# A two-layer attention and expert kernel: gates, half of the latents and both attention output projections as three float32r terms

## The chip, the cores and the metric

The kernel runs on one core of one Trainium2 chip. The metric is device microseconds of that core for one execution. Engine names are those of the profile: PE is TensorE's matmul, PEld its weight load, DVE is VectorE, ACT is ScalarE, POOL is GpSimd, SP is the engine that issues most DMAs.

## The reference

Three blocks run on a 256 x 1024 float32 activation x. The first two are layers of one kind, and the change concerns them alone:

```python
proj = x @ w_in[i]                       # 1024 -> 3*512 + 768 + 256 + 32 + 2*1024
na_qkv, q_lat, kv_lat, k_rope, g_na, g_mla = jnp.split(proj, ...)
o_na  = neighborhood_attention(q_na, k_na, v_na, na_rpb[i])     # 8 heads of 64
q_mla = rms_norm(q_lat) @ w_uq[i]; kv = rms_norm(kv_lat) @ w_ukv[i]
o_mla = latent_attention(q_mla, k_mla, v_mla)                   # 8 heads
merged = sigmoid(g_na + b) * (o_na @ w_na_o[i]) + sigmoid(g_mla + b) * (o_mla @ w_mla_o[i])
x = layer_norm(ALPHA * x + merged @ w_out[i])
f = swiglu(x) if i == 0 else moe_swiglu(x)      # layer 1: 8 experts, 2 of them per token
x = layer_norm(ALPHA * x + f + sigmoid(x @ w_ple_gate[i]) * (p[i] @ w_ple[i]))
```

A third block with other mixers and a dense feed-forward follows.

## The kernel before

The five engines run programs of their own, each in a fixed order written out by hand, and meet at semaphores. Activations lie feature-major in tiles of 128 features x 256 tokens; a projection of 1024 inputs to 128 outputs is a "tile" of eight k-steps into one PSUM bank, and two banks each are shared between PE and ACT (`act_ps`) and between PE and DVE (`dve_ps`).

**Weights** come through `weight_ring`, 7 slots of 16 KB per partition (`SLOTS`, L81). A block of up to 2 MB fills a slot. SP issues the blocks in order (L657 to L660); block i waits until PE has finished block i-7. The experts' blocks go through the same 7 slots (L632 to L636): the first seven wait for the blocks that held the slots.

**Products** come in two kinds. `product` (L817 to L826) multiplies float32 by float32. `split_product` (L911 to L920) multiplies three float32r terms per k-step, short x short, short x rest and rest x short. "short" is the operand rounded to float32r, "rest" is what is left; a half slot (128 x 2048) is a unit. Its short comes from a cast into another buffer, its rest from a subtraction in place in the ring. In the layers, the queries, keys and values (split by DVE, `split_in_w`, L1777), `w_out` and `w_ple_gate` (`layer_units`: units 0, 1, 5 by POOL, the rest by DVE) and the dense feed-forward (`split_w`, L1802, by DVE) are products of three terms already. All latents, the gates, and the output projections `w_na_o` and `w_mla_o` are float32.

**Attention** takes 16 jobs per layer, first 8 neighbourhood heads (NA), then 8 latent heads (MLA), as a software pipeline over steps s = 0 to 17. The orders within a step are:

- PE (L866): scores of job s, the gate tile s as a filler (`gate_tile`, L1153), transposes of the probabilities of job s-1, values of job s-2.
- DVE (L1699): `maxima(s)` (L1720 or L1725, then the tiny L1726), `normalise(s-1)` (L1737, then two instructions of L1747), `output(s-2)` (L1758).
- ACT (L1365): the exponentials of job s, the read of gate tile s (L1498), the copy of the transposed probabilities of job s-1.

Call E(s) the moment at which PE ends gate tile s. After step 17 PE waits for the last output and goes on with the 8 tiles of `w_na_o` and the 8 of `w_mla_o`. DVE multiplies each by its gate (L2025; L2039 and L2040 for the second, then L2032 and L2036, which split the merged tile), and the three-term `w_out` follows.

**POOL** masks the bias table of layer 0 early (L692), waits for half of the attention's maxima, loads the next bias table, splits its three units of `w_out` and `w_ple_gate`, masks again, and is free until the experts, where it makes every sixth rest (L724).

## Time and profile before

| what | value |
|---|---|
| three runs | 2307.92, 2311.07, 2311.77 us; median 2311.07 |
| profiled execution | 2307.82 us, its span 2306.0 us |
| busy in the span | PE 2204.6, PEld 1870.1, DVE 1502.4, ACT 980.5, POOL 346.0 us |
| attention of layer 0, of layer 1 (gate tiles) | about 117 to 210 us, 622 to 715 us |
| output projections | about 216 to 244 us, 721 to 749 us |
| experts | about 839 to 1780 us |

How to read it: the span is one execution on the chip; the 1.8 us between it and that execution's own time lie around it. The median of the runs lies 3.25 us above the profiled execution. A busy share is an average over stages with different limits, so the stages that the change touches are read one by one below.

### The profile page before, as it was taken

Reading aid. Unit: us, or ns where it says so; the run is one execution under the profiler, and the core shown is the slowest. Engines: PE = TensorE matmul, PEld = TensorE weight load, DVE = VectorE, ACT = ScalarE, POOL = GpSimd, SP = SyncE. Lnnn points to the kernel's source line nnn. Section 1 sums busy time; section 2 is a strip of 40 time slices with the busy share of each in tenths; the row PEclk is TensorE's granted clock in tenths of the full one; section 3 lists DMA queues with packets and bytes.
Section 4 is the critical chain, followed back from the end, with each engine's and each line's share of the span. In section 5 each row is a group of like instructions: output and inputs, shape, how many; then the busy total and the mean of one; then the engine's idle time right before and its main releaser. Section 6 shows DMA issues by size and latency. Waiting matters only on the chain.

```text
span 2306.0 us, 29557 instructions
## 1 busy us (share of the span) xinstructions
PE 2204.6 (96%) x11972; PEld 1870.1 (81%) x11972; DVE 1502.4 (65%) x1489; ACT 980.5 (43%) x1043; POOL 346.0 (15%) x95
## 2 busy tenths in 40 slices
PE   8999999989999979999999999999999798969999
PEld 7777899989777868888888888888888586648998
DVE  4342677755333568898888898988889301445776
ACT  0133210010133257777777777778776203241000
POOL 1001200000001112322323223223243000100000
PEclk9999999999999989999999999999999996979999
DMA  9532578643513459999999999999999332303530
GB/s 341 183 124 73 170 268 294 237 132 115 180 60 110 165 209 381 372 384 367 384 367 384 366 385 371 385 374 380 384 387 343 132 135 84 110 0 110 183 128 19
DMA packets 176770, 552.20 MB, mean 239 GB/s; under 512 B 11264, under 2 KB 98944, under 8 KB 133280
## 3 DMA queue, kind: packets, MB, share of 16 engines
q1 hardware_dynamic: 167984, 516.77, 60.9%
q10 hardware_dynamic: 6912, 24.97, 2.7%
q0 software_dynamic: 1776, 9.08, 1.0%
q8 instruction: 71, 1.16, 0.2%
q14 instruction: 27, 0.22, 0.0%
HBM read 527.19 MB, written 23.59 MB: 239 GB/s over the span
## 4 chain that ended last, share of the span: by engine, by line
PE 90%; DVE 6%; ACT 2%; issue 1%; DMA 1%; POOL 0%; DVEq 0%; SPq 0%; ACTq 0%; POOLq 0%
PE act_ps L990 25%; PE act_ps L825 13%; PE dve_ps L1015 12%; PE dve_ps L825 9%; PE dve_ps L918 8%; PE act_ps L918 8%; PE job_ps L951 5%; PE job_ps L825 2%; DVE weights_rest L1884 2%; PE job_ps L877 2%; PE job_ps L998 1%; PE job_ps L888 1%; PE act_ps L1126 1%; ACT expert_short L1414 0%; DVE pre_norm L1673 0%
## 5 line engine op out<-in xcount | busy, mean ns | idle before, releaser
L1884 DVE TENSOR_TENSOR weights_rest<-weight_ring,expert_short 128x2048 fp32r<-128x2048 f32 x280 | 768.2, 2784 | 113.6 <-ACT expert_short L1414 113.6
L1414 ACT ACTIVATE expert_short<-weight_ring 128x2048 fp32r<-128x2048 f32 x336 | 640.8, 1917 | 115.1 <-PE act_ps L990 75.7
L724 POOL TENSOR_TENSOR weights_rest<-weight_ring,expert_short 128x2048 fp32r<-128x2048 f32 x56 | 267.4, 4776 | 685.6 <-ACT expert_short L1414 685.6
L990 PE MATMUL act_ps<-expert_short,tokens_short 128*128 128x512 f32 x896 | 355.1, 396 | 12.0 <-DVE tokens_rest L1894 12.0
L990 PE MATMUL act_ps<-weights_rest,tokens_short 128*128 128x512 f32 x896 | 350.0, 391 | 0.0
L990 PE MATMUL act_ps<-expert_short,tokens_rest 128*128 128x512 f32 x896 | 349.9, 391 | 0.0
L1330 ACT ACTIVATE arena_mla<-act_ps 128x256 f32<-128x256 f32 (+2 forms) x89 | 34.2, 385 | 419.5 <-PE act_ps L918 346.1
L990 PEld LDWEIGHTS act_ps<-expert_short,tokens_short 128*128 128x128 f32 x896 | 168.8, 188 | 46.1 <-issue 12.3
L990 PEld LDWEIGHTS act_ps<-expert_short,tokens_rest 128*128 128x128 f32 x896 | 168.8, 188 | 36.4
L990 PEld LDWEIGHTS act_ps<-weights_rest,tokens_short 128*128 128x128 f32 x896 | 169.0, 189 | 33.7
L1813 DVE TENSOR_TENSOR weights_rest<-weight_ring,ffn_weights_short 128x2048 fp32r<-128x2048 f32 x66 | 151.3, 2293 | 2.3
L918 PE MATMUL act_ps<-ffn_in_short,ffn_weights_short 128*128 128x256 f32 x480 | 140.3, 292 | 10.3 <-DVE ffn_in_rest L2215 4.7
L1015 PE MATMUL dve_ps<-expert_short,hidden_short 128*128 128x512 f32 x448 | 139.4, 392 | 0.0
L918 PE MATMUL act_ps<-ffn_in_rest,ffn_weights_short 128*128 128x256 f32 x480 | 138.2, 288 | 0.0
L1015 PE MATMUL dve_ps<-expert_short,hidden_rest 128*128 128x512 f32 x448 | 138.1, 389 | 0.0
L1015 PE MATMUL dve_ps<-weights_rest,hidden_short 128*128 128x512 f32 x448 | 138.0, 389 | 0.0
L918 PE MATMUL act_ps<-ffn_in_short,weights_rest 128*128 128x256 f32 x480 | 137.9, 287 | 0.0
L1811 DVE CAST ffn_weights_short<-weight_ring 128x2048 fp32r<-128x2048 f32 x66 | 80.9, 1225 | 61.7 <-PE act_ps L918 33.4
L825 PE MATMUL act_ps<-residual,weight_ring 128*128 128x256 f32 x512 | 117.4, 382 | 0.0
L825 PEld LDWEIGHTS act_ps<-residual,weight_ring 128*128 128x128 f32 x512 | 95.9, 190 | 17.8 <-issue 5.3
L918 PEld LDWEIGHTS act_ps<-ffn_in_short,ffn_weights_short 128*128 128x128 f32 x480 | 94.4, 197 | 13.4 <-issue 8.6
L713 POOL TENSOR_TENSOR weights_rest<-weight_ring,ffn_weights_short 128x2048 fp32r<-128x2048 f32 x6 | 27.1, 4526 | 505.6 <-ACT ffn_weights_short L1510 505.4
(323 smaller groups left out, 3958.3 us busy)
## 6 DMA issues: line engine op xcount, KB each, us to landing
weight_ring<-in_moe_w SPq DMA_DIRECT2D x336, 1024.0 KB, 6.9
weight_ring<-in_w_in SPq DMA_DIRECT2D x44, 1024.0 KB, 7.4
weight_ring<-in_ffn_w SPq DMA_DIRECT2D x32, 1024.0 KB, 7.1
weight_ring<-in_w_out SPq DMA_DIRECT2D x12, 1024.0 KB, 6.9
weight_ring<-in_w_gate SPq DMA_DIRECT2D x11, 1024.0 KB, 5.5
weight_ring<-in_w_up SPq DMA_DIRECT2D x11, 1024.0 KB, 8.0
weight_ring<-in_w_down SPq DMA_DIRECT2D x10, 1024.0 KB, 5.9
weight_ring<-in_w_ple_gate SPq DMA_DIRECT2D x8, 1024.0 KB, 6.8
```

The lines of the kernel that those rows point to most:

```text
L724: nc.gpsimd.tensor_tensor(ring_lo[slot][:, half], ring[:, slot, half], shorts[u % SHORTS][:, :], ALU.subtract)\
L825: m = nc.tensor.matmul(out, lhs[k], rhs[k], start=first and k == 0, stop=last and k == len(lhs) - 1)
L877: m = nc.tensor.matmul(out, j["q"][:, i * P:(i + 1) * P], j["k"], start=True, stop=True)
L918: m = nc.tensor.matmul(out, a[:, k, at], x_parts[x_part][:, k, :], start=(k == i == 0), stop=(k == DT - 1 and i == 2))
L951: m = nc.tensor.matmul(acc(j), w[:, k, at], ff_h[h][:, pair % 4, k, :], start=(pair == k == i == 0 and j % 2 == 0), stop=(2 * pair + k == ...
L990: m = nc.tensor.matmul(bank[0:CAP, :], a[:, 4 * c + k, :], w[:, k, :], start=(c == k == i == 0), stop=(c == 1 and k == 3 and i == 2))
L1015: m = nc.tensor.matmul(dve_ps[n_half][0:CAP, :], h[:, g % 2, 2 * c + k, :], w[:, k, n_half * 512:(n_half + 1) * 512], start=(g == c == k = ...
L1330: nc.scalar.activation(out, bank[rows, 0:width], func, **kw).then_inc(act_tile_done, 1)
L1414: nc.scalar.activation(shorts[u % SHORTS][:, :], ring[:, slot, half], ACT.Copy).then_inc(moe_w_short, 1)
L1811: V.tensor_copy(ff_w[u % 2][:, :], ring[:, block % SLOTS, half]).then_inc(ffn_w_short, 1)
L1813: V.tensor_tensor(ring_lo[block % SLOTS][:, half], ring[:, block % SLOTS, half], ff_w[u % 2][:, :], ALU.subtract)\
L1884: V.tensor_tensor(ring_lo[slot][:, half], ring[:, slot, half], shorts[u % SHORTS][:, :], ALU.subtract)\
```

## The change

The change leaves the mathematics as it is and turns more products into the three-term kind:

- The latents' last block (4 of 8 tiles per layer), all 16 gate tiles and all 16 tiles of the two output projections become `split_product`s: 14 new units per layer, `side_units`.
- Weights: the casts of layer 0's units 0 and 1 are ACT's; all other casts and all 14 subtractions of a layer are POOL's (`split_side`). Units 0 and 1 are the latents', 2 to 9 the gates' (two tiles each), 10 and 11 `w_na_o`, 12 and 13 `w_mla_o` (four tiles each). From unit 4 on POOL waits until PE is done with unit u-2; units 11 to 13 wait for the last gate tile.
- Heads: DVE splits pairs of heads (`split_heads`: a 128 x 256 cast and a subtraction) between the steps of attention, at steps 10 to 15 and 17.
- Room: outside the experts the ring has 5 slots. Slots 5 and 6 hold the split of x (`in_x`) and the two shorts (`side_w`). Block i now waits for block i-5. The first two of the experts' blocks that go into slots 0 to 4 wait for `w_ple` and for the first block of `w_ple_gate`, the third waits for the second block of `w_ple_gate`, and SP issues all later ones behind it.
- x is split by DVE before the copies of the latents rather than between them. `w_out`'s unit 1 takes `side_w[0]` as its short, and ACT's cast for it waits for unit 10.

Cut to its core:

```diff
+LAYER_SLOTS, SIDE_UNITS = 5, 14
...
-        in_x = [parts("layer_in_short", "probs", [P, DT, SEQ]), parts("layer_in_rest", "arena_o", [P, DT, SEQ])]
+        in_x = [parts("layer_in_short", "weight_ring", [P, DT, SEQ], SLOT * LAYER_SLOTS),
+                parts("layer_in_rest", "weight_ring", [P, DT, SEQ], SLOT * LAYER_SLOTS + 2048)]
+        in_x_flat = [a[:, :, :].rearrange("p k s -> p (k s)") for a in in_x]
+        o_short = [parts(f"heads_short{i}", "arena_gate", [P, 4, SEQ], 1024 * i) for i in range(2)]
+        o_rest = [parts(f"heads_rest{i}", "arena_o", [P, 4, SEQ], 1024 * i) for i in range(2)]
+        side_w = [parts(f"side_weights_short{b}", "weight_ring", [P, 2048], SLOT * (LAYER_SLOTS + 1) + 2048 * b) for b in range(2)]
...
-            out += [(halves(panel(w, COL_GATE + 512 * i, COL_GATE + 512 * (i + 1))), "AAAA") for i in range(4)]
-            out += [(halves(panel(t["w_na_o"][l], 0, D)), "D" * DT), (halves(panel(t["w_mla_o"][l], 0, D)), "D" * DT)]
+            out += [(panels_at(w, COL_GATE + 512 * i), "AAAA") for i in range(4)]
+            out += [(column_halves(t["w_na_o"][l]), "D" * DT), (column_halves(t["w_mla_o"][l]), "D" * DT)]
...
+        def side_units(l):
+
+
+            units = []
+            for u in range(SIDE_UNITS):
+                block, c = (queries_at[l] - 1, u) if u < 2 else (ple_block_at[l] - 8 + (u - 2) // 2, u % 2)
+                a, d = tiles_before[block]
+                units.append((block, c, (dve_tile_ready, d + 2 * (c + 1)) if u < 2 else
+                              (act_tile_ready, a + 2 * (c + 1)) if u < 10 else (dve_tile_ready, d + 4 * (c + 1))))
+            return units
+
+        def side_short_of(u):
+
+            return side_w[u % 2] if u < 12 else in_x_flat[u - 12]
+
+        def layer_short_of(i):
+
+            return side_w[0] if i == 1 else ff_w[i % 2]
+
...
+            if block < before_moe:
+                return weights_here[slot], 32 * (block // LAYER_SLOTS + 1)
+            turns = len(range(slot, before_moe, LAYER_SLOTS)) + (block - before_moe) // LAYER_SLOTS + 1
+            return weights_here[slot], 32 * turns
+
+        def slot_of(block):
+
+            return (block if block < before_moe else block - before_moe) % LAYER_SLOTS
...
-                        sp.wait_ge(*blocks[before_moe - SLOTS + b][1])
+                        sp.wait_ge(*(blocks[max(range(b, before_moe, LAYER_SLOTS))][1] if b < LAYER_SLOTS
+                                     else layer_units(1)[1][2]))
...
+                if i >= LAYER_SLOTS:
+                    sp.wait_ge(*blocks[i - LAYER_SLOTS][1])
...
+            def split_side(l, u):
+
+                units = side_units(l)
+                block, c, _ = units[u]
+                half = slice(c * 2048, (c + 1) * 2048)
+                if (l, u) not in ((0, 0), (0, 1)):
+                    pool.wait_ge(*weights_landed(block))
+                    if u < 2:
+                        pool.wait_ge(*layer_units(l - 1)[1][2])
+                    else:
+                        pool.wait_ge(*units[min(u - 2, 9)][2])
+                    nc.gpsimd.tensor_copy(side_short_of(u)[:, :], ring[:, slot_of(block), half]).then_inc(side_short, 1)
+                pool.wait_ge(side_short, SIDE_UNITS * l + u + 1)
+                nc.gpsimd.tensor_tensor(ring_lo[slot_of(block)][:, half], ring[:, slot_of(block), half], side_short_of(u)[:, :],
+                                        ALU.subtract).then_inc(side_split, 1)
+
...
             for l in range(LAYERS):
-                pool.wait_ge(max_ready, layer_jobs * l + NA_H)
+                if l:
+                    for u in range(2):
+                        split_side(l, u)
+                for u in range(2, 8):
+                    split_side(l, u)
                 if l < LAYERS - 1:
+                    pool.wait_ge(max_ready, layer_jobs * l + NA_H)
                     load_bias(l + 1)
+                for u in range(8, SIDE_UNITS):
+                    split_side(l, u)
...
+                def side_weights(u):
+
+                    block, c, _ = side_units(l)[u]
+                    pe.wait_ge(side_split, SIDE_UNITS * l + u + 1)
+                    k = DT if u < 10 else 4
+                    return tiles(side_short_of(u)[:, :], k), tiles(ring_lo[slot_of(block)][:, c * 2048:(c + 1) * 2048], k)
+                for u in range(2):
+                    w = side_weights(u)
+                    for j in range(2):
+                        split_product(dve_bank()[:, 0:SEQ], w, slice(j * P, (j + 1) * P), in_x).then_inc(dve_tile_ready, 1)
+                n.block += 1
+
                 def in_weights(i):
 
...
-                    if s % 4 == 0:
-                        gate_w.append(weights(DT, 512))
-                    product(act_bank()[:, 0:SEQ], cols(gate_w[-1], s % 4 * P, (s % 4 + 1) * P), xs)\
+                    if s % 2 == 0:
+                        gate_w.append(side_weights(2 + s // 2))
+                    split_product(act_bank()[:, 0:SEQ], gate_w[-1], slice(s % 2 * P, (s % 2 + 1) * P), in_x)\
                         .then_inc(act_tile_ready, 1)
+                    if s % 4 == 3:
+                        n.block += 1
                 attention(layer_jobs * l, layer_jobs, gate_tile)
-                feature_tiles("D", weights(4, D), k_tiles(o_na, 4))
-                feature_tiles("D", weights(4, D), k_tiles(o_mla, 4))
+                for i in range(2):
+                    for c in range(2):
+                        w = side_weights(10 + 2 * i + c)
+                        for j in range(4):
+                            split_product(dve_bank()[:, 0:SEQ], w, slice(j * P, (j + 1) * P), (o_short[i], o_rest[i]),
+                                          (lambda k: (heads_split, DT * l + 4 * i + k + 1)) if c == j == 0 else None)\
+                                .then_inc(dve_tile_ready, 1)
+                    n.block += 1
                 layer_tiles(l, 0, "D", merged_parts, lambda k: (merged_split, DT * l + k + 1))
                 after = last_tiles(DT)
                 i = n.block
                 w_ple = weights(2, D)
-                p_l = tiles(ring[:, i % SLOTS, 2 * D:2 * D + 2 * SEQ], 2)
...
+            for block, c, _ in side_units(0)[0:2]:
+                act.wait_ge(*weights_landed(block))
+                nc.scalar.activation(side_w[c][:, :], ring[:, slot_of(block), c * 2048:(c + 1) * 2048], ACT.Copy)\
+                    .then_inc(side_short, 1)
...
-                    nc.scalar.activation(ff_w[i % 2][:, :], ring[:, block % SLOTS, c * 2048:(c + 1) * 2048], ACT.Copy)\
+                    if i == 1:
+                        act.wait_ge(*side_units(l)[10][2])
...
+                    if beside:
+                        beside(s)
...
+            def split_heads(l, i, j):
+
+                dve.wait_ge(out_copied, layer_jobs * l + NA_H * i + 2 * j + 2)
+                o = (o_na, o_mla)[i]
+                V.tensor_copy(o_short[i][:, j, :], o[:, j, :]).then_inc(heads_short, 1)
+                dve.wait_ge(heads_short, DT * l + 4 * i + j + 1)
+                V.tensor_tensor(o_rest[i][:, j, :], o[:, j, :], o_short[i][:, j, :], ALU.subtract).then_inc(heads_split, 1)
 
...
+                when = {10: ((0, 0),), 11: ((0, 1),), 12: ((0, 2),), 13: ((0, 3), (1, 0)), 14: ((1, 1),), 15: ((1, 2),), 17: ((1, 3),)}
+                attention(layer_jobs * l, layer_jobs, beside=lambda s: [split_heads(l, i, j) for i, j in when.get(s, ())])
```

## Rows read from the trace of the kernel before

**Rows 1.** The page: the chain that ended last, by engine

```profile
PE 90%; DVE 6%; ACT 2%; issue 1%; DMA 1%; POOL 0%; DVEq 0%; SPq 0%; ACTq 0%; POOLq 0%
```

**Rows 2.** The chain in layer 0: start us, us, what; an attention step, then the projections

```profile
156.08 0.44 PE job_ps L888 x4
...
158.58 3.65 PE act_ps L825 x16
...
170.70 3.46 PE act_ps L825 x16
...
212.05 0.63 DVE probs L1747 x2
...
215.67 27.89 PE dve_ps L825 x128
243.56 23.19 PE dve_ps L918 x192
```

**Rows 3.** Timeline of POOL, layer 0: start us, us, engine line op, releaser

```profile
266.90 1.89 POOL L709 CAST ffn_weights_short<-weight_ring 128x2048 fp32r<-128x2048 f32 x1 [36.97 <-PE dve_ps L918]
268.87 4.53 POOL L713 TENSOR_TENSOR weights_rest<-weight_ring,ffn_weights_short 128x2048 fp32r<-128x2048 f32 x1
```

**Rows 4.** Timeline of DVE, the same attention step, and two merging instructions

```profile
157.56 0.42 DVE L1758 COPY arena_o<-job_ps 64x256 f32<-64x256 f32 x1 [3.40 <-PE job_ps L825]
158.62 0.42 DVE L1720 CUSTOM_DVE_ANT_0 probs<-job_ps,arena_bias 128x256 f32<-128x256 f32 x1 [0.64 <-PE job_ps L877]
...
159.43 0.17 DVE L1726 TENSOR_SCALAR small<-small 128x2 f32<-128x2 f32 x1
...
159.70 0.61 DVE L1747 TENSOR_SCALAR probs<-probs,small 128x256 f32<-128x256 f32 x2
...
235.77 0.28 DVE L2032 CAST merged_short<-work 128x256 fp32r<-128x256 f32 x1
235.97 0.42 DVE L2036 TENSOR_TENSOR merged_rest<-work,merged_short 128x256 fp32r<-128x256 f32 x1
```

**Rows 5.** Timeline of POOL and DVE side by side, third block

```profile
1974.38 0.84 DVE L1747 TENSOR_SCALAR probs<-probs,small 128x256 f32<-128x256 f32 x2
...
1974.51 1.00 POOL L786 TENSOR_SCALAR arena_o<-arena_o,params_sb 128x256 f32<-128x256 f32 x1
...
1980.61 1.09 POOL L790 TENSOR_TENSOR arena_o<-arena_o,tmp 128x512 f32<-128x512 f32 x1
1980.83 0.89 DVE L1726 TENSOR_SCALAR small<-small 128x2 f32<-128x2 f32 x1
```

**Rows 6.** Timeline of DVE and POOL in layer 0: a cast behind the bias mask

```profile
43.62 8.88 POOL L692 TENSOR_TENSOR arena_bias<-arena_bias,consts_sb 128x3072 f32<-128x3072 f32 x1 [8.62 <-DMA arena_bias<-in_na_rpb]
...
48.01 5.58 DVE L1785 CAST layer_weights_short<-weight_ring 128x2048 fp32r<-128x2048 f32 x1 [2.20 <-PE act_ps L918]
```

**Rows 7.** Timeline of DVE: fourth latent tile, and a weight cast late in layer 0's feed-forward

```profile
22.61 0.42 DVE L1656 COPY work<-dve_ps 128x256 f32<-128x256 f32 x1 [3.03 <-PE dve_ps L825]
...
484.32 1.22 DVE L1811 CAST ffn_weights_short<-weight_ring 128x2048 fp32r<-128x2048 f32 x1
485.58 2.29 DVE L1813 TENSOR_TENSOR weights_rest<-weight_ring,ffn_weights_short 128x2048 fp32r<-128x2048 f32 x1
```

**Rows 8.** The page: weight DMAs, count, KB each, median us from issue to landing

```profile
weight_ring<-in_w_in SPq DMA_DIRECT2D x44, 1024.0 KB, 7.4
```

**Rows 9.** The chain ahead of the experts

```profile
817.53 8.54 PE act_ps L918 x48
...
829.74 5.50 ACT expert_short L1414 x3
```

**Rows 10.** Stretches: us, busy of PE, PEld, DVE, ACT, POOL, then granted clock, DMA share, GB/s

```profile
815.00:816.00 1.00, 0.00 (x0) 0.00 (x0) 0.00 (x0) 0.80 (x1) 0.53 (x1) 1.00 1.04 442
820.00:821.00 1.00, 1.00 (x7) 1.00 (x6) 0.96 (x3) 0.00 (x0) 0.00 (x0) 0.50 0.00 0
900.00:1000.00 100.00, 99.31 (x454) 81.99 (x453) 87.54 (x44) 77.19 (x53) 28.73 (x6) 1.00 0.98 380
```

More of the change, by code:

```diff
@@ L437, in two_panels, with column_halves, dmas, panels_at @@
             return pair_block(w, w, c0 // 256, c0 // 256 + 1)
+        def column_halves(w):
+            def dmas(slot):
+                return [(tiles(slot[:, i * 2048:(i + 1) * 2048], 4), panel(w, 512 * i, 512 * (i + 1))) for i in range(2)]
+            return dmas
+        def panels_at(w, c0):
+            def dmas(slot):
+                return [(tiles(slot[:, i * 2048:(i + 1) * 2048], DT), panel(w, c0 + 256 * i, c0 + 256 * (i + 1))) for i in range(2)]
+            return dmas
         def down_block(w2, g, f_tiles):
@@ L473, in layer_plan @@
             w = t["w_in"][l]
-            out = [(halves(panel(w, COL_LAT + c0, COL_LAT + c1)), "D" * ((c1 - c0) // P)) for c0, c1 in lat_blocks(l)]
+            out = [(halves(panel(w, COL_LAT + c0, COL_LAT + c1)) if i < len(lat_blocks(l)) - 1 else
+                    two_panels(w, COL_LAT + c0), "D" * ((c1 - c0) // P)) for i, (c0, c1) in enumerate(lat_blocks(l))]
             out += [(two_panels(w, COL_Q), "AAAA"), (two_panels(w, COL_K), "DDDD"), (None, "AA"),
@@ L618, in load @@
                 dmas, _ = blocks[i]
-                for dst, src in dmas(ring[:, i % SLOTS, :]):
-                    sp.dma_start(dst, src).then_inc(weights_here[i % SLOTS], 16)
+                for dst, src in dmas(ring[:, slot_of(i), :]):
+                    sp.dma_start(dst, src).then_inc(weights_here[slot_of(i)], 16)
             def load_expert_block(e, b, base):
@@ L708, in _ @@
                         pool.wait_ge(*units[i - 2][2])
-                        nc.gpsimd.tensor_copy(ff_w[i % 2][:, :], ring[:, block % SLOTS, half]).then_inc(pool_w_short, 1)
+                        nc.gpsimd.tensor_copy(layer_short_of(i)[:, :], ring[:, slot_of(block), half]).then_inc(pool_w_short, 1)
                         pool.wait_ge(pool_w_short, l + 1)
@@ L712, in _ @@
                         pool.wait_ge(act_w_short, 2 * l + i + 1)
-                    nc.gpsimd.tensor_tensor(ring_lo[block % SLOTS][:, half], ring[:, block % SLOTS, half], ff_w[i % 2][:, :],
+                    nc.gpsimd.tensor_tensor(ring_lo[slot_of(block)][:, half], ring[:, slot_of(block), half], layer_short_of(i)[:, :],
                                             ALU.subtract).then_inc(pool_w_split, 1)
@@ L913, in split_product @@
                 short, rest = w
-                for k in range(DT):
+                tiles_in = short.shape[1]
+                for k in range(tiles_in):
                     if after:
@@ L926, in layer_tiles @@
                     pe.wait_ge(*layer_unit_split(l, i))
-                    w = tiles(ff_w[i % 2][:, :], DT), tiles(ring_lo[block % SLOTS][:, c * 2048:(c + 1) * 2048], DT)
+                    w = tiles(layer_short_of(i)[:, :], DT), tiles(ring_lo[slot_of(block)][:, c * 2048:(c + 1) * 2048], DT)
                     for j in range(2):
@@ L942, in swiglu @@
                     half = slice(c * 2048, (c + 1) * 2048)
-                    short, rest = ff_w[u % 2][:, :], ring_lo[block % SLOTS][:, half]
+                    short, rest = ff_w[u % 2][:, :], ring_lo[slot_of(block)][:, half]
                     if kind == "w2":
@@ L1104, in in_weights @@
                     pe.wait_ge(in_w_split, 6 * l + i + 1)
-                    return tiles(in_w[i % 2][:, :], DT), tiles(ring_lo[block % SLOTS][:, c * 2048:(c + 1) * 2048], DT)
+                    return tiles(in_w[i % 2][:, :], DT), tiles(ring_lo[slot_of(block)][:, c * 2048:(c + 1) * 2048], DT)
                 for i in range(4):
@@ L1164, in _ @@
                 w_ple = weights(2, D)
-                p_l = tiles(ring[:, i % SLOTS, 2 * D:2 * D + 2 * SEQ], 2)
+                p_l = tiles(ring[:, slot_of(i), 2 * D:2 * D + 2 * SEQ], 2)
                 def embedding(j0, j1):
@@ L1509, in short_w @@
                     act.wait_ge(*weights_landed(block))
-                    nc.scalar.activation(ff_w[i % 2][:, :], ring[:, block % SLOTS, c * 2048:(c + 1) * 2048], ACT.Copy)\
+                    if i == 1:
+                        act.wait_ge(*side_units(l)[10][2])
+                    nc.scalar.activation(layer_short_of(i)[:, :], ring[:, slot_of(block), c * 2048:(c + 1) * 2048], ACT.Copy)\
                         .then_inc(act_w_short, 1)
@@ L1697, in rms_norm, with attention @@
                         .then_inc(rms_ready, 1)
-            def attention(first, count, fill=None):
+            def attention(first, count, fill=None, beside=None):
                 def maxima(a):
```

57 lines of the change are left out of this document (28 added, 29 removed).

## Prediction, made before the changed kernel ran

> **What bounds the kernel now.** I read the page's chain first: PE carries 90% of it [rows 1], so a PE saving is worth its full length unless something else becomes late. Then the chain in the stages that the change touches. In attention it is PE without a gap: transposes, values and scores take 2.50 us (156.08 to 158.58), then a float32 gate tile of 3.65 us with the neighbourhood heads and 3.46 us with the latent heads [rows 2]. Both output projections are 27.89 us without a gap, and the three-term `w_out` behind them 23.19 us for 8 tiles of 8 k-steps [rows 2]. Third, what DVE does within such a step [rows 4], since POOL's new work runs beside it, and what the two do to each other where they already meet [rows 5, 6].
>
> **What PE gains.** The float32 output projections are 64 k-steps in 27.89 us, 0.436 us each; `w_out` is 64 k-steps in 23.19 us, 0.362 us each [rows 2]. A three-term gate tile is then 8 x 0.362 = 2.90 us against 3.46: 0.56 us less. (The neighbourhood steps' extra 0.19 us I keep.) Sixteen gate tiles give 9.0 us a layer, the projections 64 x 0.074 = 4.7 us, four latent tiles 2.2 us. Both layers: 31.8 us, the whole of the hoped-for gain.
>
> **What POOL costs.** A unit is a cast of 1.89 us and a subtraction of 4.53 us, 6.5 us with the gap [rows 3]. PE uses a gate unit up in two steps, 11 us, so POOL is fast enough by itself. The question is DVE. L1726 works on 128 x 2 numbers and takes 0.17 us [rows 4], but 0.89 us when it starts in a POOL subtraction: it ends 0.02 us after it [rows 5]. DVE's 1.22 us cast [rows 7] took 5.58 us when it met POOL's mask: it ended 1.09 us after the mask did [rows 6]. So DVE's casts and its TENSOR_SCALAR from SBUF to SBUF wait for POOL's two-input instruction to its end. POOL can also step between two DVE instructions in a row: a pair of L1747 took 0.84 us for 0.61 with a POOL instruction started inside it [rows 4, 5].
>
> The Trainium skill, "SBUF — State Buffer", section "Who interferes with whom", says that such a pair of ports is held for the whole instruction of whoever came first. Rows 5 agree for the subtraction but not for POOL's 1.00 us TENSOR_SCALAR, which held DVE up by only 0.23 us. By the page POOL's casts block for their full 1.89 us, as below; if they held for that row's share only, the two in the tail below would cost some 3 us a layer less, and the sum would be about 2358.
>
> **A step of attention.** Let E be the end of a gate tile. From rows 2 and 4 with E = 156.08: DVE copies an output at E+1.48, starts the maxima at E+2.54, L1726 at E+3.35, L1747 at E+3.62 and ends it at E+4.23. PE needs that at the end of the next gate tile: E+6.15 now, E+5.59 after the change (E+5.40 with latent heads). The margin shrinks to 1.2 us. POOL starts a unit at an odd step's E, because PE then frees the buffer: cast to E+2.0, subtraction to E+6.6. L1726 waits from 3.35 to 6.6, and the remaining 0.9 us puts the probabilities at E+7.5: PE stalls 1.9 us (2.1 with latent heads). Units 4 to 8 do this: 3 x 1.9 + 2 x 2.1 = 9.9 us.
> At units 9 and 10 (steps 11, 13) DVE also has heads to split, a 0.28 us cast and a 0.42 us subtraction [rows 4], both blocked alike. The cast slips in between POOL's two instructions, the subtraction waits to E+6.8, the maxima start at 7.25 and 1.7 us later the probabilities are there: stall 3.5 us; with two splits at step 13, 4.2 us. Queued behind on DVE are the maxima, so ACT's exponentials come late too, but PE asks for them only a step later. Sum in attention 17.6 us a layer, against 9.0 gained.
>
> **The tail.** After E15 POOL has units 11, 12 and 13 and then two subtractions for `w_out`, 28 us with no pause, while DVE must finish. Chained as above: split cast in the gap (2.0 to 2.3), POOL subtraction to 6.8, split subtraction to 7.2, POOL cast to 9.1, first L1747 to 9.4, POOL subtraction to 13.9, second L1747 to 14.2. Today the pair starts at 212.05 and ends 2.8 us after E15, which is 170.70 + 3.46 plus six steps of 5.96 and thus 209.9 [rows 2]: 11.4 us lost. PE starts `w_na_o` at E+17.2; DVE's last head split is caught by units 13 and 14 and ends at E+25.9, and only then comes the gate product that frees PE's bank. PE has done two tiles by 20.1 and waits to 26.3: 6.2 us. With the 4.7 us gained the tail is +12.9 us. If POOL did not step between the L1747 pair it would be about +6; if nothing blocked, -4.7.
>
> **The start.** Layer 0's unit 0 needs block 2 (with x and the first blocks 5.2 MB, estimated landed at 18 to 19 us from the page's 341 GB/s of the first slice), ACT's cast (5.50/3 = 1.8 us [rows 9]) and 4.53 us on POOL: about 25 us. PE ends its fourth tile at 22.6 [rows 7]. Wait 2.4, gain 2.2: +0.2 us.
> Layer 1's units 0 and 1 need a block that is loaded when PE ends the feed-forward's fourth block from the end; it lands 7.4 us later [rows 8] and puts 13 us of POOL beside the last three weight splits of DVE, 3.5 us each [rows 7], which PE wants 5.8 us apart (48 matmuls of 0.121). A full chain of turns costs 9.5 us, a lucky one nothing; I take 5. With 2.2 gained: +2.8 us.
>
> **The ring.** Seven slots become five. Within the layers a block takes PE 11 us and DMA 7, so I cost it at nothing; the blocks ahead hide it. At the experts it shows: the third block is issued only when `w_ple_gate` is done, 826.1 [rows 9] (817.53 + 8.54), and both halves land some 7.5 us later, 833.5. ACT needs it for the second half of its shorts (from 829.74, 1.83 each [rows 9]: wanted at 831.6), and PE's start hangs on ACT. +1.9 us, between 0 and 5. After that PE takes 5.4 us per block and DMA gives 380 GB/s at a share of 0.98 [rows 10], so it keeps up, with little room.
> x's split moves ahead of the first latent copy: 3.5 us on DVE, hidden by PE's first tiles, done long before its fourth at 22.6 [rows 7]; late x could cost 1 us at most.
>
> **The clock.** After about 3 us in which PE was idle (815 to 816 wholly, until 817.53 [rows 9, 10]) the granted clock fell from 1.00 to 0.50, that is to 1.2 GHz [rows 10], and 48 matmuls took 8.54 us where 0.121 each makes 5.8 [rows 9]. Five stalls after the change are well over 3 us (two per layer in the tail, one in the feed-forward). I take 1.7 us each, between 0 and 2.7: +8.5 us.
>
> **Sum.** Per layer -9.0 + 17.6 + 12.9 = +21.5; twice 43.0; start 0.2 and 2.8; ring 1.9; clock 8.5: +56.4 us. On the profiled execution's 2307.8 us that is 2364 us. The median shown lies 3.3 us above that execution, which is inside what I can't resolve here.
>
> **Rivals.**
> A, *no harm*: POOL's instructions fall where they hold nothing up on DVE, and PE keeps its saving: -31.8, plus the ring's 1.9 and the start's wait of 2.4, is -27.5, 2280 us, faster than before. It decides at one point: whether POOL's subtraction is over by the time DVE's small L1726 plus the 1.2 us margin is up, E+4.6. POOL would have to finish 2 us sooner than rows 3 say, or DVE not to wait at all. Rows 5 and 6 speak against it; for it speaks only that they show short instructions and one cast, not a whole stage. 14%.
> B, *half the harm*: DVE waits at L1726 as in rows 5, but POOL does not step in between DVE instructions in the tail (+6 a layer, no long stall, no clock). 2 x (-9.0 + 14 + 6) + 5 = +27, 2335 us. 22%.
> C, *break-even*: B's stalls at the gates, but a tail that keeps its 4.7 us: 2 x (-9.0 + 14 - 4.7) + 5 is about +5, at the edge of no change, and a little less with fewer head splits caught. 6%.
> D, *the ring*: the experts start with an empty ring and DMA, at a share of 0.98, never fills it. Five blocks of 2 MB at 380 GB/s are 27 us, of which 13 pass before PE starts; up to 13 us more on top, 2377 us. 8%.
> The forecast, stalls plus tail plus clock: 50%.
>
> **How the numbers follow.** The predicted time is the forecast's. Range: 2310, below B, to 2390, above D with the clock at its upper bound; it leaves out A and most of C. A measurement of this kernel can tell 0.2% (4.6 us) from no change. Faster 0.15 (A and a sliver of C), same 0.05, slower 0.80.
>
> **What would show it.** In the changed profile: three-term gate tiles of 2.9 us; PE waiting at the transposes (L888's counterpart) for DVE's L1747 after every second gate tile, 2 us each; L1726 with a maximum of several us; L1747 too at the end of attention; PE idle before and inside `w_na_o`; granted clock below 1.0 in both tails. The forecast is wrong if L1726 stays near 0.2 us beside POOL's 4.5 us subtractions, or if the step of attention is 5.5 us throughout.

## The result, and the profile after

Four runs of the changed kernel took 2368.41, 2376.30, 2381.27 and 2382.16 us, median 2378.8, against 2309.5 for the kernel before beside them: 1.029 times its time, with a 95% interval of 1.026 to 1.033. The change makes the kernel 3% slower. The profiled execution is the first of the four; it is 60.6 us above that of before (2307.82).

The page's chain by engine, beside [rows 1]:

```profile
PE 85%; DVE 11%; ACT 2%; issue 1%; DMA 1%; POOL 0%; DVEq 0%; SPq 0%; ACTq 0%; POOLq 0%
```

Busy times of the engines (share of the span, instructions):

```profile
PE 2195.5 (93%) x12420; PEld 1874.7 (79%) x12420; DVE 1598.5 (68%) x1521; ACT 983.5 (42%) x1045; POOL 523.5 (22%) x149
```

PE is busy 9 us less than before and POOL 178 us more. In the chain DVE's share has nearly doubled, and POOL is as good as absent from it, though POOL is the cause: the chain names the engine whose instruction was long, not who held it up. Read alone, this row would send one to speed DVE up.

PE's waits, each with who ended them, total, count and longest:

```profile
PE job_ps L963 <- DVE probs L1849: 71.5, 22, 12.0
PE act_ps L1066 <- DVE tokens_rest L2006: 14.2, 1, 14.2
...
PE job_ps L1027 <- DVE weights_rest L1925: 9.0, 1, 9.0
```

The first wait is at the transposes, for the normalised probabilities. It grew from 13.9 us, 8 times, longest 2.6. L963 is the transposes (L888 before), L1828 the tiny negation (L1726), L1849 the normalisation (L1747).

One step of attention, DVE's timeline and then POOL's, beside [rows 4]:

```profile
146.63 0.42 DVE L1822 CUSTOM_DVE_ANT_0 probs<-job_ps,arena_bias 128x256 f32<-128x256 f32 x1
...
147.09 3.36 DVE L1828 TENSOR_SCALAR small<-small 128x2 f32<-128x2 f32 x1
150.37 0.15 DVE L1839 RECIPROCAL small<-small 128x2 f32<-128x2 f32 x1
150.55 0.61 DVE L1849 TENSOR_SCALAR probs<-probs,small 128x256 f32<-128x256 f32 x2
```

```profile
143.88 1.89 POOL L755 CAST side_weights_short<-weight_ring 128x2048 fp32r<-128x2048 f32 x1 [6.73 <-PE act_ps L994]
145.85 4.58 POOL L757 TENSOR_TENSOR weights_rest<-weight_ring,side_weights_short 128x2048 fp32r<-128x2048 f32 x1
```

POOL's subtraction ends at 150.43, and two numbers a partition take 3.36 us until 150.45. L1822, which reads PSUM, ran inside the same subtraction in its usual 0.42. The transposes that had to wait, layer 0 in order of time:

```profile
137.94 0.66 PE L963 MATMUL job_ps<-consts_sb,probs 128*128 128x128 f32 x4 [2.90 <-DVE probs L1849]
151.22 0.66 PE L963 MATMUL job_ps<-consts_sb,probs 128*128 128x128 f32 x4 [1.92 <-DVE probs L1849]
164.50 0.66 PE L963 MATMUL job_ps<-consts_sb,probs 128*128 128x128 f32 x4 [1.92 <-DVE probs L1849]
177.79 1.12 PE L963 MATMUL job_ps<-consts_sb,probs 128*128 128x128 f32 x4 [2.12 <-DVE probs L1849]
192.41 0.66 PE L963 MATMUL job_ps<-consts_sb,probs 128*128 128x128 f32 x4 [2.10 <-DVE probs L1849]
206.67 0.66 PE L963 MATMUL job_ps<-consts_sb,probs 128*128 128x128 f32 x4 [3.29 <-DVE probs L1849]
221.61 0.68 PE L963 MATMUL job_ps<-consts_sb,probs 128*128 128x128 f32 x4 [3.96 <-DVE probs L1849]
242.20 1.12 PE L963 MATMUL job_ps<-consts_sb,probs 128*128 128x128 f32 x4 [11.97 <-DVE probs L1849]
```

Five plain gate steps, two with head splits, and the end of attention; layer 1 repeats them to 0.02 us. The last one on DVE and on POOL:

```profile
230.74 0.29 DVE L1880 CAST heads_short<-arena_o 128x256 fp32r<-128x256 f32 x1
231.06 4.61 DVE L1882 TENSOR_TENSOR heads_rest<-arena_o,heads_short 128x256 fp32r<-128x256 f32 x1
235.60 0.15 DVE L1839 RECIPROCAL small<-small 128x2 f32<-128x2 f32 x1
235.79 6.36 DVE L1849 TENSOR_SCALAR probs<-probs,small 128x256 f32<-128x256 f32 x2
```

```profile
230.90 4.50 POOL L757 TENSOR_TENSOR weights_rest<-weight_ring,side_weights_short 128x2048 fp32r<-128x2048 f32 x1
235.34 2.09 POOL L755 CAST layer_in_short<-weight_ring 128x2048 fp32r<-128x2048 f32 x1
237.50 4.49 POOL L757 TENSOR_TENSOR weights_rest<-weight_ring,layer_in_short 128x2048 fp32r<-128x2048 f32 x1
```

The pair of L1849 needs 0.6 us and takes 6.36, the first 1.79 and the second 4.66: the first waits for the cast's end (237.43), POOL's subtraction gets in ahead of the second, which waits for its end at 241.99. The projections then run through. In the chain (start, us, what), beside [rows 2]:

```profile
22.41 4.50 issue
...
246.49 3.13 PE dve_ps L994 x24
249.67 43.60 PE dve_ps L994 x360
...
524.00 14.12 PE job_ps L1027 x96
...
880.76 7.20 DMA weight_ring<-in_moe_w
895.40 19.40 PE act_ps L1066 x72
```

How far after lies behind before at the same point of the program, from the two chains:

| point | before | after | behind | change in the stage |
|---|---|---|---|---|
| attention of layer 0 begins | 116.91 | 122.23 | 5.3 | +5.3 |
| output projections | 215.67 | 246.49 | 30.8 | +25.5 |
| `w_out` done | 266.75 | 293.27 | 26.5 | -4.3 |
| layer 1 begins | 513.40 | 551.47 | 38.1 | +11.6 |
| attention of layer 1 begins | 621.84 | 654.60 | 32.8 | -5.3 |
| `w_out` of layer 1 done | 771.68 | 825.74 | 54.1 | +21.3 |
| experts begin | 838.97 | 895.40 | 56.4 | +2.3 |
| end of the span | 2306.0 | 2366.3 | 60.3 | +3.9 |

Of the -5.3 the latents' three terms are 2.2; for most of the rest before had been at half clock there (granted clock 0.56 to 0.59 between 512 and 520 us; its 128 float32 matmuls took 30.89 us, where 16 take 3.45 at full clock). The last 3.9 us arise where both kernels run the same instructions, 3.4 of them behind the experts, where the mean granted clock is 0.83 (1846 to 2170 us) against 0.86 before (1790 to 2113); they were not traced further.

### The profile page after: what moved, and what is told of

Read it like the earlier page. It is cut to its first block, busy times and chain, and to the rows that moved or that the text cites. A ratio compares the mean times of both kernels' runs of the same rounds, so it can differ in the third digit from the quotient of the medians.

```text
span 2366.3 us, 30583 instructions
## 1 busy us (share of the span) xinstructions
PE 2195.5 (93%) x12420; PEld 1874.7 (79%) x12420; DVE 1598.5 (68%) x1521; ACT 983.5 (42%) x1045; POOL 523.5 (22%) x149
## 4 chain that ended last, share of the span: by engine, by line
PE 85%; DVE 11%; ACT 2%; issue 1%; DMA 1%; POOL 0%; DVEq 0%; SPq 0%; ACTq 0%; POOLq 0%
PE act_ps L1066 25%; PE dve_ps L1091 12%; PE dve_ps L994 11%; PE act_ps L994 10%; PE act_ps L900 8%; PE job_ps L1027 5%; PE dve_ps L900 5%; PE job_ps L900 3%; DVE weights_rest L1996 2%; PE job_ps L952 2%; DVE small L1828 2%; PE job_ps L963 1%; DVE heads_rest L1882 1%; PE job_ps L1074 1%; DVE probs L1849 1%
## 5 line engine op out<-in xcount | busy, mean ns | idle before, releaser
L1066 PE MATMUL act_ps<-expert_short,tokens_short 128*128 128x512 f32 x896 | 355.4, 397 | 14.2 <-DVE tokens_rest L2006 14.2
L755 POOL CAST side_weights_short<-weight_ring 128x2048 fp32r<-128x2048 f32 x22 | 42.8, 1944 | 499.2 <-DMA weight_ring<-in_w_in 326.8
L757 POOL TENSOR_TENSOR weights_rest<-weight_ring,side_weights_short 128x2048 fp32r<-128x2048 f32 x24 | 109.6, 4569 | 23.6 <-ACT side_weights_short L1579 21.9
L1027 PE MATMUL job_ps<-ffn_hidden_short,ffn_weights_short 128*128 128x256 f32 x352 | 100.9, 287 | 9.0 <-DVE weights_rest L1925 9.0
L994 PEld LDWEIGHTS act_ps<-ffn_in_short,ffn_weights_short 128*128 128x128 f32 x480 | 94.9, 198 | 13.4 <-issue 9.0
```

The source lines that it names most:

```text
L757: nc.gpsimd.tensor_tensor(ring_lo[slot_of(block)][:, half], ring[:, slot_of(block), half], side_short_of(u)[:, :], ALU.subtract).then_inc( ...
L994: m = nc.tensor.matmul(out, a[:, k, at], x_parts[x_part][:, k, :], start=(k == i == 0), stop=(k == tiles_in - 1 and i == 2))
L1027: m = nc.tensor.matmul(acc(j), w[:, k, at], ff_h[h][:, pair % 4, k, :], start=(pair == k == i == 0 and j % 2 == 0), stop=(2 * pair + k == ...
L1066: m = nc.tensor.matmul(bank[0:CAP, :], a[:, 4 * c + k, :], w[:, k, :], start=(c == k == i == 0), stop=(c == 1 and k == 3 and i == 2))
```

## The experiments

The theory (T): DVE's instructions with their operands in SBUF wait for POOL's cast or subtraction to its end. Rivals: PE waits for POOL's units themselves (W); sharing of SBUF's bandwidth (S); DVE's own added work, the head splits (H); DMA and the shorter ring (D). Ratios are to the kernel before, run beside each; its medians were 2308.7 to 2309.6 us.

**1. No subtraction (e1_no_sub).** POOL casts, but PE takes the short a second time as its third term, so that the rests of these weights are left out of the products.

```diff
+                if u >= 2:
+                    return
                 pool.wait_ge(side_short, SIDE_UNITS * l + u + 1)
                 nc.gpsimd.tensor_tensor(ring_lo[slot_of(block)][:, half], ...
```

> Left out: POOL's subtraction for the gates and both output projections (units 2 to 13); PE takes the rounded weights as the third term too, so PE's work, POOL's casts, the head splits and all transfers stay. After is 2378.8 us. Theory T (DVE's instructions between SBUF operands wait for POOL's 4.5 us subtraction to its end): the small TENSOR_SCALAR L1828 falls from 3.4 to 0.2 us and the two attention stages give back nearly all of the 2 x 34.5 us by which they run over a stall-free step: 2319 us (2308 to 2330). Rival W (PE waits because POOL's units come late): the casts alone are there sooner too, but PE's waits at the transposes would have shown POOL as the one who ends them, and they show DVE's L1849: W gives the same time here and is told apart in e2 and e3. Rival H (the eight head splits of 0.7 us are too much work for DVE): 2 x 6 us at most come back from the rest, about 2360 us.

Measured: 2306.7 us, ratio 0.999 (0.998 to 1.000). The tiny TENSOR_SCALAR is back at its 170 ns of before. DVE's instructions in 110 to 260 us, by form; after, then this run:

```profile
L1828 DVE TENSOR_SCALAR small<-small 128x2 f32<-128x2 f32 x16 | 19.8, 1239 | 0.5
```

```profile
L1833 DVE TENSOR_SCALAR small<-small 128x2 f32<-128x2 f32 x16 | 2.7, 170 | 0.6
```

With 24 instructions of POOL 72 us have gone, more than the 69 that the change had cost and 12 more than I had expected; H falls: the head splits are all still there. In the tail casts still hold DVE up, and for their whole length: three of them take 203.49 to 209.37, and the normalising pair takes 2.05 us and ends at 209.77.

**2. The same work in pieces (e2_pieces).** Casts in 4 and subtractions in 8 instructions.

```diff
-                nc.gpsimd.tensor_tensor(ring_lo[...][:, half], ring[:, slot_of(block), half], side_short_of(u)[:, :],
-                                        ALU.subtract).then_inc(side_split, 1)
+                for q in range(0, 2048, 256):
+                    at = slice(c * 2048 + q, c * 2048 + q + 256)
+                    m = nc.gpsimd.tensor_tensor(ring_lo[...][:, at], ring[:, slot_of(block), at],
+                                                side_short_of(u)[:, q:q + 256], ALU.subtract)
+                m.then_inc(side_split, 1)
```

> POOL's cast is cut in 4 pieces and its subtraction in 8, about 0.5 us each, for all 14 units; nothing is left out. Theory T: an instruction of DVE waits for one piece at most, so the small TENSOR_SCALAR takes up to 0.7 us instead of 3.4, the margin of 1.2 us mostly covers it: 2325 us (2315 to 2345; if POOL steps in between every two instructions of DVE the upper end). Rival S (both slow each other by sharing SBUF's bandwidth, whatever the length of an instruction): no change, 2379 us. Rival W (units late for PE): the pieces cost POOL 10 more instructions a unit, so 2379 or slower.

Measured: 2329.7 us, ratio 1.008 (1.006 to 1.010). S and W fall: POOL is now slower (a piece's mean is 0.78 us where an eighth of 4.57 is 0.57) and the kernel 49 us faster. What one piece costs shows in DVE's row of the same view:

```profile
L1834 DVE TENSOR_SCALAR small<-small 128x2 f32<-128x2 f32 x16 | 5.5, 343 | 0.5
```

Of the 20 us that are left, PE waits 12.6 for the merge's adds, beside POOL's two subtractions for `w_out`, which were still whole.

**3. DVE off SBUF (e3_off_dve).** POOL as in the changed kernel. ACT negates the maxima and scales the probabilities, and DVE takes both parts of the heads' outputs from PSUM.

```diff
+                        nc.scalar.activation(neg_max[:, a % 2, :], rinv[:, a % 2, :], ACT.Copy, scale=-1.0)
...
+                        m = nc.scalar.activation(probs[:, a % 2, i, :], probs[:, a % 2, i, :], ACT.Copy, scale=rinv[:, a % 2, i:i + 1])
...
+                        V.tensor_copy(short, src).then_inc(heads_short, 1)
+                        V.tensor_tensor(rest, src, short, ALU.subtract).then_inc(out_copied, 1)
```

> POOL as in the changed kernel, whole instructions. In the layers' attention DVE keeps only what reads PSUM, and the reciprocal: ACT negates the maxima and scales the probabilities (three more small ACT instructions a head), the outputs' two parts are taken straight from PSUM. Theory T: nothing of DVE in attention waits for POOL any more, both stages run at the stall-free step: 2378.8 - 69 = 2310 us (2303 to 2322). If reads of PSUM wait as well, no gain. Rival W (POOL's units late for PE) and rival D (DMA, ring of 5): 2379 us, since nothing of these changes. Rival A (ACT becomes too late): the step grows to over 6 us, 2340 us or more.

Measured: 2327.7 us, ratio 1.008 (1.006 to 1.010): 51 us of the 69. The steps of attention run at 5.6 us (5.8 with neighbourhood heads) without a wait for POOL, beside whole POOL instructions. With ACT's 1.2 us more none grows to over 6 us, so rival A falls with W and D.

The 18 us that did not come lie in two places. By the profiles attention became 26.4 us shorter in layer 0 and 28.5 in layer 1, 14 short of T's 69: the transposes take 0.63 to 0.66 us a step where a step without a wait had 0.44, PE waits for ACT's first and last probabilities (7.9 us in 4 waits), and the last head splits now stand ahead of the projections (8.2 us from the last gate tile to them, 5.8 before). The projections with `w_out` take 54.3 and 54.1 us where they took 46.8, since faster attention puts POOL's two subtractions for `w_out` beside the merge's adds:

```profile
234.03 0.41 DVE L2177 TENSOR_TENSOR tmp<-dve_ps,pre_norm 128x256 f32<-128x256 f32 x1
234.47 4.31 DVE L2178 TENSOR_TENSOR work<-work,tmp 128x256 f32<-128x256 f32 x1
```

L2177, one operand from PSUM, is not held; L2178, both from SBUF, is held for ten times its length. In the changed kernel it met none (median 0.42 us), because PE was late. PE waits here 9.0 us in all; the rest of the loss is mostly the clock (the 252 matmuls behind the wait take 33.21 and 32.15 us, 30.5 at the rate of the changed kernel's 360 in 43.60).

**4. And no latents (e6_best).** The latents' second block in float32 again, so that POOL has 12 units a layer.

```diff
-                for u in range(2):
-                    w = side_weights(u)
-                    for j in range(2):
-                        split_product(dve_bank()[:, 0:SEQ], w, slice(j * P, (j + 1) * P), in_x).then_inc(dve_tile_ready, 1)
-                n.block += 1
```

> e3 with the latents' last block in float32 again, so that POOL has no unit before the gates. Theory T: on top of e3 the wait of 4.5 us at the start of layer 0 and the 9.0 us in the last feed-forward blocks of layer 0, with 2.6 us at half clock after them, go; 2 x 2.2 us of the gain go with them: 2310 - 12 = 2298 us (2288 to 2308), that is faster than before (2309.5). What stays against before: -9.0 a layer from the gates, -4.5 a layer from the projections, +2.2 at the experts' start, which would be 2285 if nothing else is late. Rivals W and D: no faster than 2360.

Measured: 2320.0 us, ratio 1.004 (1.002 to 1.005). The 9.0 us wait in the feed-forward and the 4.5 us at the start are gone, and the profiled execution (2312.8 us) is 13 us below that of run 3 (2326.1), where 12 were expected. The medians differ by 7.7 us only: six of the ten runs had a mean granted clock of 0.959 to 0.961 and took 2320 to 2325 us, four had 0.964 to 0.966 and took 2310 to 2315. Neither level is below the kernel before: PE still waits 9.8 us for the adds of the merge. The latents cost more than they bring.

**5. Only the negation moved to ACT (e4_neg).**

```diff
-                    V.tensor_scalar(neg_max[:, b, :], rinv[:, b, :], -1.0, None, ALU.mult).then_inc(max_ready, 1)
+                        m.then_inc(max_ready, 1)
...
+                        nc.scalar.activation(neg_max[:, a % 2, :], rinv[:, a % 2, :], ACT.Copy, scale=-1.0)
```

> The changed kernel, of which only the negation of the two maxima (L1828) moves to ACT; DVE keeps the normalisation and the head splits. Theory T (every DVE instruction from SBUF to SBUF waits, whichever stands first): the 3.4 us wait moves on to the normalisation L1849, probabilities come some 0.3 us earlier in a step, 10 to 16 such steps: 2378.8 - 5 = 2374 us (2366 to 2382), and L1849's pair shows a mean of over 1.5 us. Rival F (only the small TENSOR_SCALAR is slow beside POOL): the stalls of the gate steps go, 2340 us.

Measured: 2372.2 us, ratio 1.028 (1.026 to 1.029). Rival F falls: the wait moves to the next instruction of the kind. A step on DVE, and POOL's instruction beside it:

```profile
156.59 0.16 DVE L1854 RECIPROCAL small<-small 128x2 f32<-128x2 f32 x1
156.78 3.67 DVE L1864 TENSOR_SCALAR probs<-probs,small 128x256 f32<-128x256 f32 x2
```

```profile
155.46 4.58 POOL L758 TENSOR_TENSOR weights_rest<-weight_ring,side_weights_short 128x2048 fp32r<-128x2048 f32 x1
```

The RECIPROCAL from SBUF to SBUF ran inside the subtraction, so T as I had put it ("whichever stands first") was too wide: it depends on the operation. The group's mean is 1.03 us over all 16 heads, where I had said over 1.5 for the pair.

**6. The output projections in float32 again (e5_gates)**, gates and latents as changed.

```diff
-                        w = side_weights(10 + 2 * i + c)
...
+                feature_tiles("D", weights(4, D), k_tiles(o_na, 4))
+                feature_tiles("D", weights(4, D), k_tiles(o_mla, 4))
```

> The changed kernel with both output projections in float32 again: POOL has 10 units a layer instead of 14, DVE splits no heads. This prices the projections' part. By the prediction's own terms the steps with head splits (7.7 us a layer) keep one plain stall of 2.1, and the tail's 12.9 us goes: 2 x (5.6 + 12.9) = 37 us off and two of the long stalls' clock with it: 2378.8 - 40 = 2339 us (2325 to 2348). Rival H (the projections are a gain, the gates alone are the harm): PE's 4.7 us a layer are given back, 2388 us.

Measured: 2343.7 us, ratio 1.015 (1.013 to 1.016). The projections' part was 35 of the 69 us, as the prediction's terms have it (37 without clock). Latents and gates are the other 34.

**7. Pieces for POOL's other work, the experts' slots rotated, on run 4 (e8_slots).** The pieces are cut as in run 2, the mask as in run 8.

```diff
         def moe_slot(b):
-            return b % SLOTS
+            return (b + before_moe % LAYER_SLOTS) % SLOTS
```

> e6_best (2320.0) with three things more: POOL's subtractions and casts for w_out and w_ple_gate and its mask on the biases in pieces of 256 columns (the mask: 16 pieces), and the experts' blocks rotated by three slots, so that the first of them take the slots that come free first, with all seven slots in use from the experts on. Theory T: the merge's SBUF-to-SBUF adds L2162 lose at most a piece each, so that 7 of the 9.8 us of PE's waits there go; the cast that waits 5.58 us for the mask in layer 0 falls under 2 us and PE gets 4 us of its 8; PE's wait of 13.9 us for the first tokens falls back to 12: 2320 - 7 - 4 - 2 = 2307 us (2298 to 2314). Without the blocking none of the first two helps: 2318.

Measured: 2306.3 us, ratio 0.999 (0.998 to 1.000). PE's waits for the merge's adds fell from 9.8 us to 3.8, none over 0.8, and the first tokens are there as before:

```profile
PE act_ps L1070 <- DVE tokens_rest L2026: 12.0, 1, 12.0
```

The experts' wait was no shortage of slots, then. 58 blocks precede them, so with five slots the first three of the experts' blocks had to wait for the last three of the layers'; in another order the ring is as good as with seven. By the chains the mask's pieces gave 2.9 us at the start of layer 0, where 4 were expected.

**8. The mask in pieces alone, in the kernel before (e9_mask).**

```diff
-                nc.gpsimd.tensor_tensor(flat, flat, mask, ALU.add).then_inc(bias_masked, 1)
+                for q in range(0, NA_H * BIAS_ROWS, k):
+                    m = nc.gpsimd.tensor_tensor(flat[:, q:q + k], flat[:, q:q + k], mask, ALU.add)
+                m.then_inc(bias_masked, 1)
```

> The kernel before, only with POOL's mask on the biases (L692, 8.88 us) in 16 pieces. Theory T: the DVE cast that waited 5.60 us for it (L1785) falls under 2 us, PE waits 4 us less at the start of layer 0: 2309.5 - 4 = 2305.5 us (2303 to 2308). Rival: something else (the copy that frees the bank, the block's DMA) keeps PE where it is, 2309.5.

Measured: 2307.2 us, ratio 0.9996 (0.9985 to 1.0006), which a measurement can't tell from no change. The cast went from 5.58 us [rows 6] to

```profile
48.43 1.56 DVE L1788 CAST layer_weights_short<-weight_ring 128x2048 fp32r<-128x2048 f32 x1 [2.21 <-PE act_ps L921]
```

and attention began at 114.38 instead of 116.91: 2.5 us, where I had expected 4. PE had been idle only 2.7 us there (the window of 50 to 60 us in the trace of before has it busy for 7.26); the rest of the cast's wait had lain beside a tile.

**9. The second layer's mask whole again, the merge's rounding on ACT, on run 7 (e10_act_merge).**

```diff
-                    V.tensor_copy(merged_parts[0][:, j, :], merged[:, j, :]).then_inc(merged_short, 1)
+                    nc.scalar.activation(merged_parts[0][:, j, :], merged[:, j, :], ACT.Copy).then_inc(merged_short, 1)
```

> e8_slots (2306.3) with two things more: the second layer's mask as one instruction again (in pieces it kept one SCALAR_TENSOR_TENSOR of DVE, L1782, for 4.78 us, where the three together took 2.07 in e6_best), and the rounding of the merged tiles by ACT instead of DVE, which takes one SBUF-to-SBUF instruction a tile out of the stage in which DVE and POOL still meet. Theory T: -4 us from the first, and up to 1.9 us of PE's wait in 224 to 236 us in each layer from the second: 2306.3 - 6 = 2300 us (2296 to 2305), ratio to before 0.996. If pieces were not the reason for the 4.78 us, or ACT's part comes too late for DVE: 2306.

Measured: 2302.6 us, ratio 0.997 (0.996 to 0.998): 0.3% below the kernel before, with an interval that leaves out 1. Between 224 and 236 us PE is busy 11.50 us where it was 10.11. Three SCALAR_TENSOR_TENSORs that took 5.56 us beside the mask's pieces take 3.45 us beside the whole one, which is over in 6.69 us where the pieces took 8.79:

```profile
270.56 3.45 DVE L1785 SCALAR_TENSOR_TENSOR pre_norm<-pre_norm,params_sb,std 128x256 f32<-128x256 f32 x3
```

**10. The same with the output projections in float32 (e11_gates_off).**

```diff
+                feature_tiles("D", weights(4, D), k_tiles(o_na, 4))
+                feature_tiles("D", weights(4, D), k_tiles(o_mla, 4))
```

> e10_act_merge with both output projections in float32 again (DVE copies the heads' outputs whole, POOL has 8 units a layer and then the two for w_out). What the projections' three terms are worth once nothing waits: PE gives 4.7 us a layer back, POOL is done 26 us earlier and the merge loses nothing to it (1 to 3 us a layer back), the end of attention has one DVE instruction less: e10 + 2 x (4.7 - 2.5) = 2304 us (2300 to 2309). Rival: POOL's load in the tail still costs more than the projections gain, so it is below e10, 2297.

Measured: 2299.4 us, ratio 0.996 (0.995 to 0.998). It is not slower than run 9, as I had expected, but 3 us below it; the two intervals overlap, so their order stays open. With DVE out of the way, three terms for the output projections bring nothing that the medians show. In the profiles of layer 0 (last gate tile to the end of `w_out`) they are 1.4 us shorter, 55.6 against 57.0: of PE's 4.3 us, 1.1 are lost at the end of attention (7.3 us to the projections against 6.3), the rest in the projections and the merge. In layer 1 they are 0.2 us longer, 57.3 against 57.0, at a mean granted clock of 0.79 against 1.00 between 700 and 716 us.

## Why the prediction was right, and where not

The direction, the mechanism and the place were right; 2364 us was forecast, and 2368 was the profiled execution, 2379 the median. Step by step:

- **PE's gain** as forecast for the tiles: in the chain gate tiles are 2.88 and 3.07 us. The projections with `w_out` took 46.8 us, 4.3 less, where 4.7 were forecast.
- **Gate steps**: 1.9 and 2.1 us a stall were forecast; 1.92, 1.92, 2.12 and 2.10 came. The first (2.90) was larger: its step had no values yet for PE to multiply (1.01 us in the others). The transposes behind a wait took 0.66 us instead of 0.44, 1.5 us a layer, for which the forecast had no term. Steps with head splits: 3.5 and 4.2 forecast, 3.29 and 3.96 measured. Together 18.2 us a layer against 17.6. Runs 1, 3 and 5 show that the wait for POOL is the cause, and the Trainium skill's page "SBUF — State Buffer", section "Who interferes with whom", holds here. It says that a DVE instruction in a two-port mode (copy, cast and tensor_scalar can enter one), or one with two SBUF inputs beside a GpSimd instruction that reads SBUF, contends with GpSimd, that whoever comes first has the ports for its whole instruction, and that one with at most one SBUF input outside these modes does not contend. L1828 (3.36 us for 0.17) and L2178 (4.31 for 0.42) waited, L1822 and L2177 (0.42 and 0.41) did not. The POOL instruction of [rows 5] that the forecast calls a subtraction is an add of two operands in SBUF; the reading holds for it too. The casts hold for their full length too (run 1), so the alternative sum by the row of POOL's 1.00 us TENSOR_SCALAR [rows 5] is refuted.
- **End of attention**: 11.4 us forecast. E15 was at 228.79 in the chain, the second L1849 ended at 242.15, 13.4 us later against 2.8 before: 10.6.
- **The stall of 6.2 us inside `w_na_o` did not come**; this step failed. I had unit 13 and POOL's next subtraction, the first for `w_out`, catch the last head split until E+25.9. In the trace unit 13 caught the split's cast (2.22 us for 0.28), but its subtraction was over at 248.55 and the split at 249.16 (E+20.4), before PE had used up the bank's slack, and POOL's next instruction began only at 250.86, as ACT's shorts for `w_out` came late. The stage changed by -4.3 us where I had +1.5.
- **The starts** were undersized: +0.2 and +2.8 forecast, +5.3 and +6.3 measured (11.6 - 5.3). PE waited 4.5 us for unit 0, not 2.4: POOL's subtraction of it began at 22.31, where my sum had it begin at about 20.5, and two groups of 96 matmuls took 13.23 and 13.26 us instead of 11.52 (granted clock 0.63 in 28 to 32 us, 0.72 in 56 to 60). At the end of layer 0's feed-forward the full chain of turns came, 9.0 us, of which I had taken 5; and the matmuls behind it ran 96 in 14.12 us instead of 11.52. Run 4 took both waits out (13 us in the profiles).
- **The ring**: +1.9 forecast, +2.2 measured (14.2 against 12.0), by the named chain: the third block lands at 887.96 (880.76 + 7.20) and ACT waits for it. Run 7 removed it by order alone.
- **The clock**: 8.5 us forecast, 15 found in the chain, of which 3.4 at the start, 2.6 in the feed-forward and 4.5 in each attention (1.5 in the step below, 1.6 behind the wait of 3.96 us, 1.4 behind that of 11.97). The step behind the fourth plain stall, in the chain:

```profile
177.79 1.12 PE job_ps L963 x4
178.91 1.90 PE job_ps L900 x4
180.81 1.25 PE job_ps L952 x4
```

At full clock the three are 0.66, 1.01 and 1.06. The granted clock is 0.50 in 178 to 180 us, that is 1.2 GHz. The length of the wait before does not tell by itself: behind 2.12 us here and 3.96 at 221.61 the clock had fallen, behind 2.10 at 192.41 and 3.29 at 206.67 it had not. The forecast counted only stalls of well over 3 us. The kernel before had lost 3.2 us in this way at the start of layer 1, which the changed one does not. The mean granted clock of the profiled execution is 0.958 (0.973 before); the other three runs had 0.951 or 0.952 and were 8 to 14 us longer. That is why the median is above the forecast; what the clock cost in each of them was not traced.

So the time came out close partly by luck. Against the forecast of 56.4 us the starts were 8.6 us dearer and attention 11.0, and 3.9 came at the end; the stage of the projections was 11.6 cheaper, and the 8.5 for the clock are inside these stages. Rivals A to C fall with the 1.9 us stalls and the 10.6 in the tail, D with the 2.2 us.

## What to carry to other kernels

Before work is given to an idle POOL, list DVE's instructions that would run beside it by where their operands lie: those with an operand in PSUM lost nothing here, a 128 x 2 TENSOR_SCALAR from SBUF to SBUF took 3.4 us, and its place in a pipeline with 1.2 us of margin decides. If the work must be POOL's, take the sensitive instructions off DVE (ACT, or an operand straight from PSUM; 51 of 69 us here) or cut POOL's into pieces (49 us, for about a third more POOL time). And when one stage is sped up, look at what the next now meets: the merge's adds had been safe only because PE was late.

## What had not been expected

- A RECIPROCAL of DVE from SBUF to SBUF ran in 0.16 us inside POOL's subtraction (run 5), where a TENSOR_SCALAR of the same 128 x 2 waited 3.36 us.
- POOL gets in between two DVE instructions issued back to back (a 0.6 us pair took 6.36 us), but DVE does not always get in between POOL's. In run 7 the mask's 16 pieces of 0.55 us stood back to back from 269.15 to 277.94, and DVE's first three SCALAR_TENSOR_TENSORs, begun at 273.45, took 5.56 us to 279.01; in run 2 one piece was the most that the tiny TENSOR_SCALAR waited. The same pieces in layer 0 did let DVE's casts and subtractions in (run 8, 15 of the 16 in its trace: 1.56 us for 1.22, 2.57 for 2.29) and were drawn out themselves, which speaks for the operation; no run tried it alone:

```profile
44.18 16.35 POOL L694 TENSOR_TENSOR arena_bias<-arena_bias,consts_sb 128x192 f32<-128x192 f32 x15 [8.75 <-DMA arena_bias<-in_na_rpb]
```

- POOL waits for DVE as well. The whole mask took 8.88 us in the kernel before [rows 6], where it began 0.11 us into a subtraction of DVE, and 6.82 in the changed kernel, where DVE's next instruction came 1.86 us later. DVE before, then POOL after:

```profile
43.51 2.29 DVE L1787 TENSOR_TENSOR weights_rest<-weight_ring,layer_weights_short 128x2048 fp32r<-128x2048 f32 x1
```

```profile
44.15 6.82 POOL L742 TENSOR_TENSOR arena_bias<-arena_bias,consts_sb 128x3072 f32<-128x3072 f32 x1 [8.04 <-DMA arena_bias<-in_na_rpb]
```

- ACT's added instructions in attention (0.2 us for 128 x 2, 0.5 us for 128 x 256) beside POOL's subtractions left the steps at 5.6 to 5.8 us. PE waited for ACT only at the two ends of the stage (run 3: 7.9 us in 4 waits).
